# A new order for the latent norm, the decay stage and the row broadcasts in a two-block kernel

## The reference, cut to what matters

```python
h = rmsnorm(x, norm_gain); proj = h @ w_in
(gq, gk, gv, gb, ga, gz, mq, mkv, mkr, mz, lx, lz) = split(proj)
# a: gated delta rule, 4 heads of 128
qkv = silu(causal_dwconv(concat([gq, gk, gv]), gdn_conv_w))
q, k = l2norm(q), l2norm(k)
beta = sigmoid(gb); g = -exp(a_log) * softplus(ga + dt_bias)
gc = cumsum(g); decay = exp(where(tril, gc[:, None] - gc[None, :], -inf))
o_a = rmsnorm(gated_delta_rule(q, k, v, g, beta), out_norm) * silu(gz)
# b: latent attention, 8 heads
qm = rmsnorm(mq, mla_q_norm) @ w_uq; kv = rmsnorm(mkv, mla_kv_norm) @ w_ukv
o_b = causal_softmax_attention(rope(qm), rope(kv)) * silu(mz)
# c: gated linear recurrence over time
u = causal_dwconv(lx) + b; r, i = sigmoid(u @ w_r), sigmoid(u @ w_i)
a = exp(-8 * r * softplus(-a_param)); h_t = a_t * h_{t-1} + sqrt(1 - a_t**2) * i_t * u_t
o_c = h * silu(lz)
x = x + concat([o_a, o_b, o_c]) @ w_out
```

## Time and profile before

| | us |
|---|---|
| median of three runs | 1642.65 (1640.84 to 1644.35) |
| profiled execution, its own time | 1642.59 |
| its span, first to last instruction | 1640.8 |
| TensorE busy | 1569.6 (96%) |
| VectorE busy | 1029.2 (63%) |
| ScalarE busy | 893.3 (54%) |
| GpSimd busy | 65.0 (4%) |

### The profile page before, as it was taken

The page is one execution under the profiler, slowest core; times in us unless marked ns, Lnnn a source line. Parts: engine busy times, 40 slices in busy tenths (PEclk is TensorE's granted clock), DMA queues, the critical chain, the costliest instruction groups (busy, mean ns, idle before and its releaser), DMA issues.

```text
span 1640.8 us, 24598 instructions
## 1 busy us (share of the span) xinstructions
PE 1569.6 (96%) x10174; PEld 1359.6 (83%) x10174; DVE 1029.2 (63%) x1599; ACT 893.3 (54%) x1419; POOL 65.0 (4%) x58
## 2 busy tenths in 40 slices
PE   7989999998989999999989999989999999899999
PEld 7989877998877788889977888878888888678887
DVE  6877675796766755545785655456555556765454
ACT  5986464686565545446446544445454456654442
POOL 0013000011200000000000000000000000000000
PEclk9999999999999999999999999999999999999999
DMA  7624224542413666555423556544665553246552
GB/s 231 204 71 144 78 102 137 180 143 72 154 53 121 200 207 196 186 180 165 146 91 107 188 186 199 180 130 154 205 200 182 184 163 120 78 156 197 186 183 100
DMA packets 203616, 252.55 MB, mean 154 GB/s; under 512 B 17136, under 2 KB 183280, under 8 KB 203376
## 3 DMA queue, kind: packets, MB, share of 16 engines
q1 hardware_dynamic: 203504, 250.97, 47.7%
HBM read 249.90 MB, written 1.05 MB: 153 GB/s over the span
## 4 chain that ended last, share of the span: by engine, by line
PE 78%; DVE 11%; ACT 7%; issue 2%; DMA 1%; SPq 0%; POOL 0%; DVEq 0%; ACTq 0%; POOLq 0%
PE bank L802 75%; ACT arena L1487 4%; DVE weights_rest L2039 3%; DVE arena L2187 2%; ACT weights_high L1487 1%; PE bank L1250 1%; DMA ring<-in_w_in 1%; ACT L1482 1%; ACT L1487 1%; DVE xT_rest L2433 1%; DVE small L2361 0%; PE bank L1184 0%; PE bank L859 0%; DVE x L2402 0%; DVE weights_rest_more L2039 0%
## 5 line engine op out<-in xcount | busy, mean ns | idle before, releaser
L2039 DVE TENSOR_TENSOR weights_rest<-ring,weights_high 128x1024 fp32r<-128x1024 f32 (+2 forms) x410 | 474.0, 1200 | 173.0 <-ACT weights_high L1487 171.1
L1487 ACT ACTIVATE weights_high<-ring 128x1024 fp32r<-128x1024 f32 (+2 forms) x410 | 398.7, 1026 | 133.8 <-PE bank L802 116.8
L802 PE MATMUL bank<-weights_high,xT_high 128*128 128x512 f32 (+1 forms) x864 | 330.5, 387 | 8.8 <-DVE xT_rest L2433 3.5
L802 PE MATMUL bank<-weights_high,xT_rest 128*128 128x512 f32 (+1 forms) x800 | 301.5, 377 | 0.0
L1487 ACT ACTIVATE arena<-bank 128x512 f32<-128x512 f32 (+5 forms) x316 | 142.9, 471 | 266.6 <-PE bank L802 256.8
L802 PE MATMUL bank<-xT_high,weights_high 128*128 128x256 f32 (+1 forms) x936 | 275.2, 294 | 4.7 <-DVE xT_rest L2133 2.4
L802 PE MATMUL bank<-xT_rest,weights_high 128*128 128x256 f32 (+1 forms) x936 | 268.2, 287 | 0.0
L802 PE MATMUL bank<-xT_high,weights_rest 128*128 128x256 f32 (+1 forms) x904 | 258.8, 286 | 0.0
L802 PE MATMUL bank<-weights_rest,xT_high 128*128 128x512 f32 (+1 forms) x680 | 256.4, 381 | 0.0
L802 PEld LDWEIGHTS bank<-weights_high,xT_high 128*128 128x128 f32 x864 | 162.4, 189 | 42.0 <-issue 5.0
L802 PEld LDWEIGHTS bank<-xT_high,weights_high 128*128 128x128 f32 (+1 forms) x936 | 181.6, 194 | 10.2 <-issue 4.6
(11 more groups left out here) (187 smaller groups left out, 1956.7 us busy)
## 6 DMA issues: line engine op xcount, KB each, us to landing
ring<-in_w_in SPq DMA_DIRECT2D x36, 1024.0 KB, 5.3
ring<-in_ffn_w_gate SPq DMA_DIRECT2D x71, 512.0 KB, 4.0
ring<-in_ffn_w_up SPq DMA_DIRECT2D x71, 512.0 KB, 5.0
ring<-in_ffn_w_down SPq DMA_DIRECT2D x34, 1024.0 KB, 4.9
ring<-in_w_out SPq DMA_DIRECT2D x22, 1024.0 KB, 4.9
ring<-in_w_in_a SPq DMA_DIRECT2D x11, 1024.0 KB, 5.3
ring_more<-in_ffn_w_down SPq DMA_DIRECT2D x10, 1024.0 KB, 5.0
ring_more<-in_ffn_w_gate SPq DMA_DIRECT2D x17, 512.0 KB, 4.0
```

The source lines that it names most:

```text
L802: return eng.matmul(o, a, b, start=first, stop=last)
L1487: return eng.activation(dst, src, func, **kw_)
L2039: TTs(rest_slot(b)[:, part], raw_slot(b)[:, part], high_slot(key)[:, part].bitcast(F32), ALU.subtract).then_inc(*dv.mark(("rest", key, z)))
```

## The change

Three stages of the list move, in both layers. `("mla_norm", l)` goes from behind `("silu", l, 2)` to behind `("lru_c", l)`. `("decay", l)` goes from behind `("silu", l, 1)` to behind `("l2", l, 0)`, so that the SiLU of half 1 stands right before `proj("lz", 0)`. `("decay_b", l)` goes from behind `proj("gv", 1)` to before it. As `rn` is now written by the latent norm before the first norms, ScalarE's `st_l2` waits for the latent multiplies where it waited for nothing, and its `st_mla_norm` no longer waits for the second norms' products. Nothing else differs.

```diff
--- before.py
+++ after.py
@@ -161,9 +161,9 @@
             return ("proj", l, name, j)
 
         out += [proj("lx", 0), ("abt", l), proj("lx", 1), proj("mq", 0), proj("gq", 0), ("lru", l), proj("mq", 1)]
-        out += [proj("gq", 1), ("lru_b", l), proj("mkv"), ("silu", l, 0), proj("gk", 0), ("lru_c", l)]
-        out += [proj("gk", 1), ("l2", l, 0), proj("gv", 0), ("silu", l, 1), ("decay", l), proj("lz", 0), proj("gv", 1)]
-        out += [("decay_b", l), ("l2", l, 1), proj("lz", 1), ("silu", l, 2), ("mla_norm", l), proj("gz", 0), ("vT", l)]
+        out += [proj("gq", 1), ("lru_b", l), proj("mkv"), ("silu", l, 0), proj("gk", 0), ("lru_c", l), ("mla_norm", l)]
+        out += [proj("gk", 1), ("l2", l, 0), ("decay", l), proj("gv", 0), ("silu", l, 1), proj("lz", 0), ("decay_b", l), proj("gv", 1)]
+        out += [("l2", l, 1), proj("lz", 1), ("silu", l, 2), proj("gz", 0), ("vT", l)]
         out += [("gdn_a", l, n) for n in range(2)]
         rots = [("rot", l, i) for i in (4, 0, 1, 2, 3)]
         beside = {2: ([("uq", l, 0)], [("uq", l, 1)]), 4: ([("uq", l, 2)], [("uq", l, 3)]),
@@ -1740,8 +1740,7 @@
                 for p in (2 * half, 2 * half + 1):
                     g = ("l2", l, p)
                     ac.wait_ge(*at(g))
-                    if p >= 2:
-                        ac.wait_ge(*at(("qk", l, p - 2)))
+                    ac.wait_ge(*at(("qk", l, p - 2) if p >= 2 else ("mla32", l, 1)))
                     r = rn[:, p % 2, :, :]
                     rsqrt(r, ps(g, 2, S), 1, True, frees=g, extra=-0.5 * np.log(128.0) if p < 2 else 0.0, key=("rn", l, p))
 
@@ -1755,8 +1754,6 @@
                 l = st[1]
                 g = ("mn", l)
                 ac.wait_ge(*at(g))
-                ac.wait_ge(*at(("qk", l, 2)))
-                ac.wait_ge(*at(("qk", l, 3)))
                 v = ps(g, 2, S)
                 A(rn[:, 0, 0, :], v[:, 0, :], ACT.Ln, scale=1.0 / 384, bias=small_eps(), fine=True).then_inc(*ac.mark(frees=g))
                 ac.wait_ge(*ac.last())

```

## The result

| | before | changed |
|---|---|---|
| median, us | 1642.98 (4 runs, 1640.84 to 1644.35) | **1629.6** (4 runs, 1628.63 to 1631.42) |
| ratio | | 0.9922 [0.991, 0.9934] |
| profiled execution, its own time | 1642.59 | 1629.73 |
| span | 1640.8 | 1628.0 |

A forecast was written before the change was run, and what follows sets the result against it. ScalarE's late eviction of gz 0's bank, stopping TensorE before Q, was taken as the bound. Per layer 5.5 us plus slow clock gave 7.4 and 8.3, together 15.7; 1642.6 less 15.7 is 1626.9, forecast 1627.0, range 1621.5 to 1635.

The forecast's parts named there:

- Case A: The forecast itself: gz 0's bank comes in time for TensorE's Q products, 1627.0 us; chance 0.74.
- Table loads: ScalarE, before `decay` and the gates of lz 0 and gz 0: three loads of 1.30 us fewer a layer, 3.9 us.
- The wait at the masks: ScalarE at `decay_b`, waiting for VectorE's masks: 3.63 us before, taken as 0.5 after the change.
- The wait for GpSimd's square: TensorE before the latent norm's products, layer 1: about 0.4 us of new wait, out of the 1.26 at `vT`.
- The bank: gz 0's bank, needed for Q: free at 109.9 instead of 118.08, asked for at 112.6, 2.7 us to spare.
- The two terms of the gain: Q starts 5.5 us earlier in each layer; slow clock saved up to the end of `gz` 1, 1.9 us in layer 0.
- `vT` starts where it did: End of the stage: ScalarE, 7 us later at the keys, is level at the values' SiLU; layer 1's 1.26 us wait stays.
- GpSimd's share: VectorE slowed beside GpSimd's moved squares: nothing to 2 us a layer, 0.2 taken.
- the second pair of key squares: GpSimd, on gv 0's conv and lz 1's weights: costs VectorE 1 to 2 us; by the skill's lock, up to 3.
- B: Rival: the wait moves to before lz 0 or `vT`, 2 to 3 us a layer; 1634 to 1636 us; chance 0.15.
- C: Rival: gain given back behind `gz` 1, or the order has no effect on the bank; 1641 to 1643 us; chance 0.06.
- D: Rival: slower, ScalarE blocked at `decay_b` ahead of gv 1 until VectorE's masks; 1648 us if 11 us late; chance 0.05.

The follow-up runs named there:

- `vT` late: Against the changed kernel, the transposes of v (`vT`) stand behind both `gdn_a` stages instead of before them; 1628.44 us.
- the split: Against the changed kernel, GpSimd's latent square is cut in two, the mq part done earlier, at `lru_b`; 1629.23 us.
- both: Against the changed kernel, the latent square is cut in two and the transposes of v stand behind `gdn_a`; 1628.14 us.
- without the square: Against the changed kernel, GpSimd squares 16 columns instead of 1280 for the latent norm, whose results are not the reference's; 1627.43 us.

## Why the prediction was right, and where its sum was off

**Case A came true**: the bank is free in time, in both layers, and the time fell by more than the 0.2% that can be told, within the range, 2.6 us above the number. What follows takes the points in the order of the prediction.

- **What bounds the kernel** was read rightly: ScalarE's lateness at the end of the stage, through the bank of gz 0. In all eight orders the waits of TensorE over 1.1 us in this stage are for ScalarE, here or at an earlier place.
- **Table loads** as forecast, three a layer, 1.30 each. That the two saved by the decay stage are worth nothing by themselves in the old order is shown by that stage alone.
- The Trainium skill (ScalarE: Activation LUTs, What ACT_TABLE_LOAD costs) would have had 2.66 us for each. The rows speak for 1.30: after the load at 72.37 the next activation starts at 73.66.
- **The wait at the masks**, forecast 0.5, is 0.49. **VectorE's wait of 5.68 us** before the latent multiplies is gone. **The wait for GpSimd's square** in layer 1, forecast 0.4, is 0.61.
- **The bank** was forecast free at 109.9. Eviction of gz 0 starts at 110.75, so it is free near 111.3. The Q products start at 114.31 (the row at 113.42 and 0.89 for its first eight), 3 us later, against the 2.7 to spare of the forecast. The lateness of ScalarE did not use up this margin, because `vT`, and with it Q, was late by as much.
- **The two terms of the gain** can be set apart. From `vT` to the Q products it was 118.13 - 108.16 = 9.97 us in layer 0. Now it is 4.45 (eight products, 0.9, behind the ones that start at 113.42): 5.52 won in each layer, forecast 5.5. From Q to the end of `gz` 1 it was 9.29 and 10.11, and is 7.09 and 7.10: 2.2 and 3.0 won, forecast 1.9 and 2.8.
- **The step that failed** is "`vT` starts where it did", through two statements: "VectorE's four scans end at 74.15 to 74.24, so its five multiplies need not wait", and GpSimd's share, taken at 0.2 us a layer. The latent square was put "beside gk 1's weights, which have 3 us to spare". They have, on TensorE. But VectorE works in order, and behind the weights stand the conv and the scans, and behind these the multiplies for which ScalarE waits. The slack there was only VectorE's idle 1.37 us between the pairs of halves. The price was 8.44 - (2.35 + 3.30) = 2.79, less 1.36: 1.43 us. As ScalarE had no slack to `vT` either, all of it arrived: `vT` is 1.69 - 0.24 = 1.45 us late in layer 0 and 1.47 in layer 1, where VectorE's step behind `lru_b` is 6.21 us earlier than it was (323.64 against 329.85) and `vT` only 4.74. In the repeat of the changed kernel TensorE shows no wait before `vT` in layer 1, and yet starts it at 374.47, as here at 374.62. It was held up by half clock in gv 1 (granted 0.50 from 355 to 358 us, with TensorE busy throughout; 8.66 us to lz 1's first product instead of 7.18), and was through gz 0 just when the values' SiLU ended, at 374.3. ScalarE sets this time in both, and the spell was hidden in its wait.
- **The whole**: 15.7 forecast; less 1.45 and 1.47; plus 0.5, since the stretch from Q to the end of `gz` 1 takes 7.1 at full clock and not the 7.35 of the sum; less about 0.5, which the kernel gives back behind layer 1 (the end of `gz` 1 is 399.44 - 386.17 = 13.3 us earlier, the span 12.8): 12.8.
- The page on SBUF (the Trainium skill: SBUF — State Buffer, Who interferes with whom) has a lock that blocks the loser for a whole instruction. The prediction drew "up to 3 us" from it for the second pair of key squares. These take 2.25 us at 91.57 and cost gv 0's conv 3.75 - 3.08 = 0.67 and lz 1's differences 3.08 - 2.35 = 0.73, 1.4 us together, inside the 1 to 2 us drawn from the rows. That the price in the other place, 2.79 us, comes near 3 is luck; that such a price would appear at `vT` was said rightly, for the wrong squares. Nor do the rows look like a lock: both engines slow down, the latent square from 2.38 to 2.85 us, the next squares from 3.02 to 3.89, and 6.74 us of squares lengthen the differences by 3.7.

```profile
91.57 2.25 POOL L2723 TENSOR_TENSOR arena<-arena 128x512 f32<-128x512 f32 x2 [23.47 <-ACT arena L1487]
```

```profile
92.95 3.08 DVE L2036 TENSOR_TENSOR weights_rest<-ring,weights_high 128x1024 fp32r<-128x1024 f32 x2
```

- **Rivals.** B is what happens when the moves are made in part: 4.82 us before `vT` (latent norm alone), 5.11 before the row broadcasts (latent norm and rows), 1639 and 1642 us. It is there in small in the changed kernel too. Of C there are the 0.5 us given back behind layer 1. D did not occur; `decay_b` ahead of gv 1 is by itself a gain of 5.8 us.
- Not foreseen at all was how the parts depend on each other: -3.1, +0.3 and -5.8 alone do not add up to 13.4 or 13.9, and two of three can give nothing. I argued each step as if the others stood, which was right for the sum of all, and wrong by 10 us for a part of them (1627 expected without the latent norm, 1637.42 measured).

## What to carry to other kernels

In an order that every engine walks without passing a wait, slack belongs to an engine and a place: before work of a helper engine is put "beside" something, follow the slowed engine's own list to the next operation for which someone waits. Saved work on an engine (table loads here) is worth only what is left of it at the engine's next wait. When several stages move together, test subsets before you drop one as useless: the decay stage alone gained nothing, and the two other moves without it gained nothing either, where all three gain 13 us.

## What the runs showed of the hardware

- **Gaps and clock.** After a gap of TensorE of 1.36, 1.61 or 2.64 us the eight transposes took 1.07, as without a gap. After 4.82 they took 1.94. Eight products took 1.16 after 1.71 us, 1.87 after 3.19, and 2.08 after 5.35. So the length of the gap alone does not order them (1.16 after 1.71, but 1.07 after 2.64). The clock differs even behind the same gap: at about 274 us every kernel has a gap of 3.31 or 3.32 us, and the eight transposes behind it took 1.09 in six of the thirteen executions and 1.97 in four. And it fell to 0.50 in gv 1 where TensorE had not waited (the changed kernel again, `vT` late). What came before in both is the spreading of the rows over the partitions, products of four rows and 2 us in all, but the first execution of the changed kernel and those with the split, with both and without the square have these too and kept 1.00 in gv 1. Why it fell is open. The sum had a cost of the clock for 5.35 us alone, the only long gap in the stages that it covers.
- **VectorE beside GpSimd.** 6.74 us of squares cost the four differences of 1.2 us each 8.44 - 4.7 = 3.7 us, and were themselves 1.3 us longer than the same squares in the old run. So the price falls on both sides.
- **A stretch that the edits leave nearly alone** took 200.6 to 203.2 us in seven profiled executions. The five slower ones are those in which the clock fell behind the wait at 210 us. Differences below some 2 us in this kernel need more runs than were made here.
